# A hybrid decoder layer on one core: the second feed-forward's up projection in token order, by one level of Strassen's scheme, with the weight block sums made in place by VectorE

## What is computed

```python
def swiglu(h, w_in, w_out):
    u, v = jnp.split(h @ w_in, 2, axis=-1)
    return (jax.nn.silu(u) * v) @ w_out
...
x = x + 0.5 * swiglu(rmsnorm(x, norm_ffn1[l]), ffn1_w_in[l], ffn1_w_out[l])
x = x + hybrid_mixer(rmsnorm(x, norm_mix[l]), ...)
x = x + 0.5 * swiglu(rmsnorm(x, norm_ffn2[l]), ffn2_w_in[l], ffn2_w_out[l])
return rmsnorm(x, norm_final)
```

## Time and profile before

| | before |
|---|---|
| median of 3 runs | 1171.47 us (1171.19 to 1171.48) |
| profiled execution: span | 1170.0 us, about 1.5 us under the median of the runs |
| TensorE matmul busy | 1155.9 us, 99% |
| VectorE busy | 553.7 us, 47% |
| ScalarE busy | 390.2 us, 33% |
| granted TensorE clock, mean | 0.997 |
| transfers | 111.47 MB, mean 95 GB/s |

### The profile page before, as it was taken

The page is one execution under the profiler, slowest core; times in us unless marked ns, Lnnn a source line. Parts: engine busy times, 40 slices in busy tenths (PEclk is TensorE's granted clock), DMA queues, the critical chain, the costliest instruction groups (busy, mean ns, idle before and its releaser), DMA issues.

```text
span 1170.0 us, 16754 instructions
## 1 busy us (share of the span) xinstructions
PE 1155.9 (99%) x6863; PEld 952.8 (81%) x6863; DVE 553.7 (47%) x834; ACT 390.2 (33%) x515; POOL 159.2 (14%) x190
## 2 busy tenths in 40 slices
PE   9999999999999999999999999999999999999997
PEld 6888888888888988877778888888888888888886
DVE  6544344463223466566776444553544434432113
ACT  6323323232223133443445422333532332321112
POOL 1000000000111472346770000021000000000000
PEclk9999999999999999999999999999999999999999
DMA  7332333323335931424132133333333233222221
GB/s 230 108 108 75 104 108 81 87 74 99 99 99 134 203 91 45 95 52 80 45 81 54 48 99 91 108 108 90 108 108 103 77 108 107 77 103 80 100 72 72
DMA packets 192229, 111.47 MB, mean 95 GB/s; under 512 B 31984, under 2 KB 186016, under 8 KB 192176
## 3 DMA queue, kind: packets, MB, share of 16 engines
q1 hardware_dynamic: 187616, 104.97, 33.0%
q0 software_dynamic: 4400, 5.61, 1.9%
q10 hardware_dynamic: 160, 0.14, 0.0%
HBM read 105.71 MB, written 2.10 MB: 92 GB/s over the span
## 4 chain that ended last, share of the span: by engine, by line
PE 95%; DVE 3%; issue 0%; DMA 0%; ACT 0%; SPq 0%; ACTq 0%; DVEq 0%
PE ps L1391 22%; PE ps L1392 21%; PE ps L1393 21%; PE ps L1547 3%; PE ps L1546 3%; PE ps L1548 3%; PE ps L1473 3%; PE ps L1474 3%; PE ps L1475 3%; PE ps L1625 2%; PE ps L1669 1%; PE ps L1698 1%; PE ps L1423 1%; PE ps L1425 1%; PE ps L1429 1%; PE ps L1644 1%
## 5 line engine op out<-in xcount | busy, mean ns | idle before, releaser
L984 DVE TENSOR_TENSOR w_lo<-w_raw,w_hi 128x2048 fp32r<-128x2048 f32 (+5 forms) x111 | 223.6, 2014 | 386.2 <-ACT w_hi L722 385.9
L1391 PE MATMUL ps<-xg_hi,w_hi 128*128 128x512 f32 x936 | 367.4, 393 | 0.0
L1393 PE MATMUL ps<-xg_hi,w_lo 128*128 128x512 f32 x936 | 364.4, 389 | 0.0
L1392 PE MATMUL ps<-xg_lo,w_hi 128*128 128x512 f32 x936 | 364.4, 389 | 0.0
L722 ACT ACTIVATE w_hi<-w_raw 128x2048 fp32r<-128x2048 f32 (+3 forms) x99 | 179.4, 1812 | 377.2 <-PE ps L1393 230.6
L1391 PEld LDWEIGHTS ps<-xg_hi,w_hi 128*128 128x128 f32 x936 | 175.7, 188 | 37.5 <-issue 1.6
L1393 PEld LDWEIGHTS ps<-xg_hi,w_lo 128*128 128x128 f32 x936 | 175.7, 188 | 36.6
L1392 PEld LDWEIGHTS ps<-xg_lo,w_hi 128*128 128x128 f32 x936 | 175.8, 188 | 35.7
L1473 PE MATMUL ps<-w_hi,p_hi 128*128 128x512 f32 x176 | 69.2, 393 | 0.0
L764 ACT ACTIVATE tmp_a<-tmp_a 128x512 f32<-128x512 f32 x44 | 27.8, 632 | 124.2 <-DVE tmp_a L1046 124.2
L1475 PE MATMUL ps<-w_hi,p_lo 128*128 128x512 f32 x176 | 68.6, 390 | 0.0
(11 more groups left out here) (221 smaller groups left out, 1369.5 us busy)
## 6 DMA issues: line engine op xcount, KB each, us to landing
w_raw<-in_ffn_w_in SPq DMA_DIRECT2D x86, 512.0 KB, 5.1
w_raw<-in_w_in SPq DMA_DIRECT2D x32, 512.0 KB, 5.2
w_raw<-in_ffn_w_out SPq DMA_DIRECT2D x22, 512.0 KB, 4.1
w_raw<-in_ffn_w_out SPq DMA_DIRECT2D x16, 384.0 KB, 3.5
w_raw<-in_w_in SPq DMA_DIRECT2D x24, 256.0 KB, 4.5
w_raw<-in_ffn_w_out SPq DMA_DIRECT2D x16, 320.0 KB, 4.0
w_raw<-in_w_out SPq DMA_DIRECT2D x8, 512.0 KB, 4.5
x_nat<-in_x SPq DMA_DIRECT2D x8, 256.0 KB, 4.8
```

The costliest lines, as they stand in the source:

```text
L984: lo = V.tensor_tensor(w_lo[:, s, c], w_raw[:, s, c], w_hi[:, s, c].bitcast(F32), ALU.subtract)
L1391: mm(out, ah, bh, start=(first and i == 0), stop=False)
L1392: mm(out, ah, bl, start=False, stop=False)
L1393: last = mm(out, al, bh, start=False, stop=(final and i == len(pairs) - 1))
```

## The change

The up projection of the second feed-forward is turned around and cut by blocks. Tokens become the stationary operand and weights stream, so that products come with tokens on the partitions. The 1024 x (n gate columns and n value columns) of a *unit* are seen as a 2x2 block matrix (two halves of K by value or gate), and the activations as 2x2 blocks too (halves of the tokens by halves of K). One level of Strassen's scheme in Winograd's form then needs seven block products instead of eight. There are six units: unit 0 with n = 256, units 1 to 5 with n = 512. One product (one *operand*, `o` = 0 to 6) is 2 token groups x 4 K tiles x 3 passes = 24 matmuls of n columns.

- The weight sides of the seven products are B11, B12-B22 (`dve_diff`), B21, T1 (`dve_t1`), B22, T2 (`dve_t2`) and T4 (`dve_t4`). Four of them are sums, made by VectorE in the buffers that hold the raw blocks; -B11 is made by ScalarE (`act_minus`). All seven are then converted to hi and lo in two halves each (`act_op`, `dve_op`).
- The activation sides `a_hi`, `a_lo` (A11, S3, A12, S1, S4, S2, A22) are made once, most of them during the output projection (`act_operands`, `dve_operands`), the last ones within unit 0 (`act_late_operands`, `act_late_squares`, `dve_late_operands`).
- Products are put together by additions on VectorE (v11, w7, w5, e1, u12, y, v21) and copies on ScalarE (`act_chain`); silu and the gate product follow (`prod1`, `prod2`), with `rstd` now one number per partition. `pe_col` and `pe_row` fall away.
- The gate product has tokens on the partitions, and the down projection needs it the other way: TensorE transposes it (`pe_turn`), and it is split (`act_turned`, `dve_turned`).
- Down now runs in three segments D0, D1, D2, each after two units (`SEGMENTS`). Its 528 matmuls stay; its partial results are added to `x_nat` after each segment (`dve_add`).
- The residual is transposed by `pe_nat` during the output projection, and the final norm reads `x_nat` rather than PSUM.
- Buffers get fixed places. The raw buffers of the second feed-forward are five (`raws`: two halves of `w_raw`, and raw_98, raw_99, raw_100 in the rows below, for r = 2, 3, 4).

```diff
+        for kind, n in (("U", 0), ("U", 1), ("D", 0), ("U", 2), ("U", 3), ("D", 1), ("U", 4), ("U", 5), ("D", 2)):
+            SEGMENTS.append((kind, n, OPS))
+            OPS += 7 if kind == "U" else 4
...
+        OPERAND = (B11, B_DIFF, B21, B12, B22, B_MINUS, B21)
...
+        def dve_t1(dve, i, u):
+            dve.wait_ge(S["minus"], u + 1)
+            dve.wait_ge(S["diff"], u + 1)
+            V.tensor_tensor(raw_of(u, B12), raw_of(u, B12), raw_of(u, B_MINUS), ALU.add).then_inc(S["t1_ready"], 1)
...
+        def act_late_squares(act, i):
+            act_nat(act, i, 7)
+            act_nat_squares(act, i, 1)
+            act_a_hi(act, i, A22, 0)
...
+        def pe_unit(pe, i, u, g0):
+            S, n = up_sems[i], cols_of(u)
+            for o in range(7):
+                sl = (FFN2 + g0 + o) % 2
+                for g in range(2):
+                    pe_bank_free(pe, i, u, o, g)
+                    bank = up_bank("first" if o in (2, 6) else "second" if o == 4 else "chain", g, u)
+                    for k in range(4):
+                        if g == 0 and k % 2 == 0:
+                            pe_op_ready(pe, i, g0 + o, k // 2)
+                        if g == 0 and u == 0:
+                            pe.wait_ge(S["a_lo"], a_index(o, k) + 1)
+                        wh, wl = (w[:, sl, k * n:k * n + n] for w in (w_hi, w_lo))
+                        ah, al = a_hi[o][:, k, g, :], a_lo[o][:, k, g, :]
+                        goes_on = o in (1, 3, 5)
+                        mm(bank, ah, wh, start=(k == 0 and not goes_on), stop=False, skip_group_check=goes_on)
+                        mm(bank, ah, wl, start=False, stop=False, skip_group_check=goes_on)
+                        last = mm(bank, al, wh, start=False, stop=(k == 3), skip_group_check=goes_on)
+                    last.then_inc(S["product"], 1)
+                    if u == 0 and o == 0 and g == 0:
+                        pe_nat(pe, i, 7)
+                if u % 2 and o < 2:
+                    pe_turn(pe, i, u - 1, o)
...
         def dve_final(dve):
-                if tt == TT - 1:
-                    dve.wait_ge(fin_squares, TT)
-                    V.tensor_tensor(tmp_a[:, :], ps[:, b, :], gain_row[:, 0, :], ALU.mult).then_inc(fin_gained, 1)
...
+            for tt in range(TT):
+                dve_add(dve, 1, 2, 1, tt)
+                if tt:
+                    scaled(tt - 1)
+            scaled(TT - 1)
```

More of the change, by code:

```diff
@@ L295, in build @@
                      ("unit_done", "gate_scaled", "value_scaled", "silu_ready", "prod_ready", "prod_hi",
-                      "prod_lo")} for i in range(2)]
+                      "prod_lo")} for i in range(1)]
+        raw_landed = [sem(f"ffn_raw_landed_{r}") for r in range(5)]
+        up_sems = [{n: sem(f"up{i}_{n}") for n in
+                    ("xs_ready", "sum_ready", "a_hi", "a_lo", "nat_psum", "nat_ready", "nat_squared",
+                     "minus", "diff", "t1_ready", "t2_ready", "t4_ready", "op_hi", "op_lo", "product", "down",
+                     "chain_copied", "v11", "w7", "w5", "e1", "u12", "y", "v21", "silu12", "silu22", "prod1", "prod2",
+                     "transposed", "p_hi", "p_lo", "added")} for i in range(1, 2)]
+        up_sems.insert(0, None)
         proj_psum = sem("projection_in_psum")
@@ new lines, in act_down @@
+        def act_down(act, i, d, g0):
+            S, u = up_sems[i], 2 * d + 1
+            ends = after("D", d) is None
+            act_op(act, i, g0 + 1)
+            for half in range(2):
+                for g in range(2):
+                    act_turned(act, i, u, half, g)
+            act_op(act, i, g0 + 2)
+            if ends:
+                nc.scalar.activation(warm[:, :], ones[:, 0:1], ACT.Sqrt)
+            act_op(act, i, g0 + 3)
+            if not ends:
+                act_op(act, i, g0 + 4)
@@ new lines, in dve_down @@
+        def dve_down(dve, i, d, g0):
+            u = 2 * d + 1
+            ends = after("D", d) is None
+            for g in range(2):
+                dve_v21(dve, i, u, g)
+            dve_op(dve, i, g0 + 1)
+            for g in range(2):
+                dve_prod2(dve, i, u, g)
+            for half in range(2):
+                for g in range(2):
+                    dve_turned(dve, i, u, half, g)
+            dve_op(dve, i, g0 + 2)
+            for tt in range(TT):
+                dve_add(dve, i, d, 0, tt)
+            dve_op(dve, i, g0 + 3)
+            if not ends:
+                dve_diff(dve, i, u + 1)
+                dve_op(dve, i, g0 + 4)
+                for tt in range(TT):
+                    dve_add(dve, i, d, 1, tt)
@@ new lines, in pe_op_ready, with pe_turn @@
+        def pe_op_ready(pe, i, g, half):
+            pe.wait_ge(up_sems[i]["op_lo"], 2 * g + half + 1)
+        def pe_turn(pe, i, u, half):
+            S = up_sems[i]
+            for g in range(2):
+                pe.wait_ge(S["prod2" if half else "prod1"], 2 * u + g + 1)
+                if half or u:
+                    pe.wait_ge(S["p_lo"], 4 * u + g + 1 if half else 4 * u - 2 + g + 1)
+                for k in range(ktiles_of(u)):
+                    last = nc.tensor.transpose(ps[:, 6 + g, k * P:k * P + P], lane(u, g, 1 if half else 3)[:, k * P:k * P + P],
+                                               ident)
+                last.then_inc(S["transposed"], 1)
```

832 lines of the change are left out of this document (655 added, 177 removed).

## The result

| | before | after |
|---|---|---|
| median of 4 runs each | 1171.47 us (1171.19 to 1172.12) | 1164.51 us (1162.95 to 1164.84) |
| ratio | | 0.9939 (95%: 0.9925 to 0.9953) |
| profiled execution: span | 1170.0 us | 1162.8 us |
| granted TensorE clock, mean | 0.997 | 0.994 |

The change makes the kernel 0.6% faster, 7.0 us by the medians and 7.2 by the spans. The prediction was 1163, 1.5 us too low.

What follows compares the result with a forecast made beforehand. TensorE was taken as the bound, busy 1155.9 of 1170.0 us. -20.9 + 1 + 8.5 + 2.7 = -8.7 gave 1161.3, plus 1.5 for runs above the profile: 1163 us, range 1156 to 1174.

Steps and rivals of the forecast that it cites:

- Matmuls removed and added: Up projection on TensorE: old matmuls out, seven-product matmuls and 88 transposes in; -20.9 us if nothing waits.
- VectorE keeps up in units 1 to 5: Full units: VectorE needs 87 to 90% of TensorE's time; +1 us over five units and D0's start.
- the rival of the other sign: Full units: conversions at 1477 ns make VectorE the bound; +15 us, 1178; chance 0.15 slower, 0.05 near the old time.
- Unit 0 waits 8.5: Unit 0 and the start of unit 1: TensorE waits behind late work, 8.5 us in sum, bounds 3 and 14.
- the residual copy: Unit 0, between the halves of operand 0: TensorE waits 0.9 us for ScalarE's copy of residual tile 5.
- operand 3: Unit 0: TensorE waits 2.9 us before this operand, behind ScalarE's residual tile, four sums of squares, A22 and two copies.
- operand 6: Unit 0: TensorE waits 1.4 us before this operand, behind VectorE's `dve_rstd` and e1.
- unit 1: Starts 2.9 us late, behind full-width difference, four sums, silu with a table load, and a full-width conversion.
- The clock: Rival: TensorE's clock falls in unit 0; 1165 to 1168 us, chance 0.13.
- rule weighed: Idle TensorE drops to half rate, so unit 0's operands take 5.8 instead of 2.9 us; +2 to +4, 1165 to 1167.
- the case without the fall: Likeliest case, as worked out: waits of 6 to 12 us, clock not lowered; 1159 to 1166 us, chance 0.55.
- The tail: Final norm: last scaling starts 6.1 us after the last product, against 3.4; +2.7 us, bounds 1 and 4.

Runs made afterwards that it cites:

- the last run: Changed kernel with five edits together: late squares, unit 1's difference, a product copy, a D0 split and the final norm's order moved; 1158.72 us, ratio 0.9894.
- the base: The changed kernel run again with no edit, as yardstick for the edited versions; 1165.23 us, ratio 0.9945 to the kernel before.

## Why the prediction came out as it did

- **Matmuls removed and added, -20.9.** Right: the stretches without waits (units 2 to 5 and D1, 201.2 us) come out at the prices of the earlier trace rows, the eight-product run gives 24 matmuls at 5.44 us, and the ledger with this term closes to 0.2 us.
- **VectorE keeps up in units 1 to 5.** Right in units 2 to 5: no wait, where up to 0.5 per unit was allowed. A conversion of 1024 takes 1221 ns there, the 1216 of the earlier trace rows and not the 1477 of the mixer, so the rival of the other sign fell. It was nearer than it looked. In units 2 and 3 VectorE is idle for 8 of 77.94 us, but the list can take only 0.3 us more per unit where the slack was worked out as 1, and the run with 14 us more on VectorE is slower than before. The 1 us allowed for it was small for unit 1 and D0: 1.4 us lie in D0, 0.6 of them before transposes of turned products, and 0.2 in unit 1 beside its clock.
- **Unit 0 waits 8.5.** Right in its causes and nearly so in its terms: the residual copy 0.6 (said 0.9), operand 3 2.3 (2.9), operand 6 1.0 (1.4), unit 1 3.0 (2.9). These are 6.9 of the 8.2 us lost without the clock; most of the rest is that a wait costs some 0.2 us beyond its length (the starts around the 2.32 us wait lie 2.60 apart and the next one 0.19). That the wait at operand 3 comes from the squares with A22 and the one at unit 1 from the full-width difference was shown by moving each.
- **The clock**, the term that the sum left out. The "rule weighed" had put its price at +2 to +4 and its chance at 0.13. It happened: 2.7 us, 1.1 in unit 0 and 1.6 in unit 1, shown by filling the waits. The step that failed is the choice, by the 2.0 us of the earlier trace rows, to take the case without the fall as the likeliest. Those waits were read for their length and not for the clock behind them: of the two, 2.0 and 1.91 us, the second had the fall in the trace of before, which the prediction could have seen. In the six us from 812 and from 830 the granted clock was 0.72. The Trainium skill, page "TensorE: Matmul & The Clock Gate", part 1, has an idle TensorE throttled to half rate; the trace agrees, with sixteen matmuls of 256 columns 0.213 us apart instead of 0.12, and eight of 512 columns 0.424 apart instead of 0.227 (8 x 0.2 is the 1.6). The price had been given as what shows of operands twice as long, some half of 3 us at each place: the size was right, the chance was not.
- **The tail, +2.7.** Measured 2.2, with a round of VectorE of 2.95 instead of 3.1. ScalarE's order holds 0.9 of it, by the last run (6.0 to 5.1 us); that the rest is VectorE's round is read from the timeline and was not tested by itself.
- **Why 1163 was still near.** From first addition to last scaling the gain is 2.4 us less than the 8.7 predicted: 2.7 for the clock, 0.6 in unit 1 and D0 without it and 0.1 ahead of unit 0, against 0.3 in unit 0 and 0.5 in the tail that were allowed for and not lost; 0.2 stay unexplained. The stretch ahead of the first addition, where the change does nothing, was 0.8 shorter in this execution by the clock in the mixer. That leaves 1.6, and the median missed by 1.5. That the miss is not larger is in part luck; the base, six runs of the same kernel, missed by 2.2.

## What to carry over

A pipeline of small pieces in front of one of large pieces needs its late work kept out of the small ones: the same block sum that costs nothing in a unit of 38 us delays the next unit by its full length in one of 20. A long wait of TensorE (here those from 1.9 us on) should be priced twice, as itself and, with a chance, as the slow matmuls after it; look at the granted clock behind each long wait of the old trace first. Where the wait can't be removed, spare matmuls buy back the second part. When an instruction is moved in an ordered list, look at everything it now stands before; the moved squares, the moved difference and the moved final square each brought a wait or a longer round elsewhere (1.3 us, 1.4 us, 0.25 us per round).

## What the hardware showed unexpectedly

The clock's fall is not the same in every execution. After the wait of 3.0 to 3.1 us before unit 1 it fell in each of the five profiles that had it whole. After the 2.3 us wait in unit 0 it fell in the changed kernel, its repeat, the run with eight products and the one with the moved final square, and stayed at 1.00 in the runs with the moved difference, with more VectorE work and with cut sums, which had the same wait. Of the two 2.16 us waits in the run with more VectorE work, the clock stayed after the one that ended at 978.6 us and fell after the one that ended at 1106.8. In the mixer it fell once in every profile, that of the kernel before too: in seven after the first of two waits, 1.92 to 2.63 us long there, and in four not after the first, 2.00 to 2.64 long there, but after the second of 1.91. So a stall of this length costs 1.1 to 1.6 us or nothing, and runs of one kernel scatter by it.

The fall doesn't come with the wait either: in unit 0 the matmuls from 812.95 to 813.67 us, right behind the 2.3 us wait, still came 0.12 us apart, and the slow ones followed. What decides was not found. Length alone does not. In the seven profiles with the 2.3 us wait in unit 0, the four in which it ended at 812.8 us or later had the fall and the three in which it ended at 812.3 or earlier had none; no run tests whether the place in time is the cause.
